# One more tile pair per layer in seven products, token sums built block by block, and 512-column weight tiles moved by 192 bytes

## The chip, the core and the metric

The kernel runs on one core of one Trainium2 chip. The metric is the device time of one execution in microseconds. The engines are TensorE (PE in the profile, with its weight loads as PEld), VectorE (DVE), ScalarE (ACT), GpSimd (POOL) and the DMA queues, most of them issued by SyncE (SP). A difference of about 1% (10 us) is what a measurement of this kernel can tell from no change.

## The reference

A causal decoder trunk of two layers over 512 tokens of width 1024, in float32. What is computed in layer i:

```python
z = rmsnorm(h, norm_mix_pre[i])
z = mlstm_mixer(z, ...) if i == 0 else swa_sink_mixer(z, ...)
h = h + rmsnorm(z, norm_mix_post[i])
z = conv_ffn(rmsnorm(h, norm_ffn_pre[i]), f_w_up[i], f_conv_w[i], f_conv_b[i], f_w_down[i])
h = h + rmsnorm(z, norm_ffn_post[i])

def conv_ffn(h, w_up, conv_w, conv_b, w_down):
    gate, val = jnp.split(h @ w_up, 2, axis=-1)          # 2 x 2816 columns = 2 x 22 tiles of 128
    gp = jnp.pad(gate, ((0, 0), (CONV_W - 1, 0), (0, 0)))
    gate_c = conv_b + sum(conv_w[j] * gp[:, j:j + S] for j in range(CONV_W))
    return (jax.nn.silu(gate_c) * val) @ w_down
```

The mLSTM mixer projects q, k, v, an output gate and head gates, runs a chunked recurrence and projects out. The attention mixer is grouped-query attention in a window of 128 tokens, with 16 query and 2 key heads.

## The kernel before

**Precision.** Every float32 matmul is made as three passes over a split of both operands: w = w_hi + w_lo and z = act_hi + act_lo, each half rounded to float32r, and w_hi z_hi + w_hi z_lo + w_lo z_hi summed in PSUM. ACT makes each hi (a cast), DVE each lo (a subtraction with both inputs in SBUF). `act_hi` and `act_lo` hold the normed and transposed tokens, [128, 8, 512].

**Weights.** SP loads tiles of 128x1024 into four buffers `raw`; ACT and DVE split them into eight slots of `w_hi` and `w_lo`. The list `SLOT` gives the slot of each tile g, and counting semaphores (`w_hi_done`, `w_lo_done`, `w_used`) keep the order. Between `w_lo` and `act_hi` lies a tile `skew` of 48 floats, so that everything above it stands 192 bytes off the 512-byte grid of the weights. All loops are written out in order; no planner places work.

**Matmuls of 512 columns.** `project` (L1825 to L1833, weights stationary, tokens moving) in its full width, `first_units` (L1851 to L1869), `v_unit` (L1894 to L1917), `out_part` (L2014 to L2029) and `down_part` (L2111 to L2118), the last three with weights moving. In the loop of the down projection the stationary operand is `hid_pair`, which lies in slot 2 of the same weight tiles; in its last four tiles it is `act_hi` and `act_lo`. The halves of `project` and all of the seven products have 256 columns.

**The up projection** makes, for each of 22 tiles f, a pair: gate tile and value tile. The first four pairs are plain (`PLAIN = 4`): pairs 0 and 1 for the first 256 tokens, then for the last 256 (eight half units), pairs 2 and 3 in units of 512 columns. The other 18 pairs (`SEVENS`) take seven products each (L2090 to L2109): the 2x2 blocks over (input half, token half) of gate and value are formed by a Strassen scheme. A product is 4 steps of k x 3 passes with 256 columns. They need
- sums of tokens `t1` to `t4` (`t_sums`), made by DVE from `act_hi` and `act_lo` in `first_sums` (L1500 to L1511) and `last_sums`, then split as `t_hi_form` (ACT, `form_hi`) and `t_lo_form` (DVE, `form_lo`, L1524);
- sums of weights, made by POOL in `weight_sums` (L604 to L618): four additions of 128x512, with both inputs in SBUF. For pair (m, t) they wait until PE is done with the tiles whose slots they overwrite: `pool.wait_ge(w_used, m * 4 + counted(up + 2 * t - 3))`. ACT and DVE split them (`raw_hi`, `sum_hi`; `raw_lo`, L1533 and L1536, `sum_lo`, L1549).

**Order around a pair.** ACT and DVE work on pair f while PE makes the products of the next one. `conv` or `conv_taps` are two DVE operations (L1468, L1472) from PSUM, `silu` (L853) is ACT's, `gated_val` (L1482) writes `hid`. In `seven(m, t, nm, nt, pm, pt)` ACT's order is: `raw_hi` of the next pair, `part 0`, `silu` of the previous pair, `raw_hi`, `part 1`, `part 2`, `sum_hi`, `part 3`, `sum_hi`. PE waits for `part 0` before its third product, `part 1` before its fourth, `part 2` before its fifth.

Of the kernel before, what the change touches and what calls it, by code (L numbers as in the profile page):

```python
# [24 lines left out]
F32 = mybir.dt.float32  # L25
# [5 lines left out]
P = 128  # L31
# [8 lines left out]
def trunk(nc, x, x_turned, columns, m_w_in, m_gate_bias, m_w_out, a_w_in, a_sinks, a_w_out,  # L40
# [34 lines left out]
    PLAIN = 4  # L75
    SEVENS = FT - PLAIN
    SKEW = 48
    HT = S // 2
    QW = KT // 2 * P
    assert FT % 2 == 0 and PLAIN == 4  # L80
# [7 lines left out]
    FFN_SLOTS = [4 + n % 4 for n in range(2 * PLAIN)]  # L88
    FFN_SLOTS += [(0, 1, 6, 7)[n % 4] for n in range(2 * SEVENS)] + [n % 2 for n in range(FT - TAIL)]
# [8 lines left out]
    DMAS[G_GATE] = 0  # L98

# [20 lines left out]
    with ExitStack() as ctx:  # L120
# [6 lines left out]
        def below():  # L127
# [22 lines left out]
        KB = 256  # L150
# [10 lines left out]
        t_last_sum = nc.alloc_sbuf_tensor_at("t_last_sum", [P, D], F32, offset=t_last_at + 4 * D)  # L161
        t_early = nc.alloc_sbuf_tensor_at("t_early", [P, 4, D], F32R, offset=arena_at + 4 * 48 * KB)
# [59 lines left out]
        hid = arena[:, 0:44 * KB].rearrange("p (f t) -> p f t", f=FT)  # L222
        cv = arena[:, 44 * KB:48 * KB].rearrange("p (b t) -> p b t", b=2)
# [6 lines left out]
                              for w in (w_hi, w_lo))  # L230

# [9 lines left out]
        wg_pack = w_hi[:, 7].rearrange("p (k c) -> p k c", k=KT)  # L241
# [39 lines left out]

        t_sum, t_form_hi, t_form_lo = sem("t_sum"), sem("t_form_hi"), sem("t_form_lo")
# [107 lines left out]
        def unit(slot):  # L390
            return (w_hi[:, slot].rearrange("p (k c) -> p k c", k=KT),
                    w_lo[:, slot].rearrange("p (k c) -> p k c", k=KT))
# [154 lines left out]
        def _(pool):  # L547
# [81 lines left out]
            nc.gpsimd.tensor_tensor(w_lo[:, s], raw[:, s % 4], w_hi[:, s].bitcast(F32),  # L629
                                    ALU.subtract).then_inc(w_lo_done, 1)  # L630
# [11 lines left out]
        def _(act):  # L642
# [7 lines left out]
            def split_hi(g):  # L650
# [4 lines left out]
                nc.scalar.copy(w_hi[:, s], raw[:, s % 4]).then_inc(w_hi_done, 1)  # L655
# [45 lines left out]
            for k in range(KT):  # L701
# [4 lines left out]
                if k >= 1:  # L706
                    act.wait_ge(raw_in[m], 16)
                    nc.scalar.copy(w_hi[:, m, cols], raw[:, m, cols]).then_inc((even_hi, w_hi_done)[k % 2], 1)
# [125 lines left out]
            norm_pre(2 * NB - 1, NB - 1)  # L834
# [1540 lines left out]
```

## Time and profile before

| | us |
|---|---|
| three runs | 1044.77, 1052.29, 1052.50 (median 1052.29) |
| the profiled execution, its own time | 1044.88 |
| its span (first to last instruction) | 1043.0 |
| PE busy | 1034.1 (99%) |
| DVE busy | 712.0 (68%) |
| ACT busy | 540.8 (52%) |
| POOL busy | 288.1 (28%) |

In 40 slices PE is at nine tenths or more in all but the last one. DVE is at eight to nine tenths in the slices in which the up projections run, at three to seven tenths elsewhere. The granted TensorE clock is full throughout (mean 0.999). A matmul row's duration includes its pipeline, so the distance from start to start is the measure of what one costs. The profiled execution is 7.4 us shorter than the median of the three runs and agrees with the shortest of them.

### The profile page before, as it was taken

To read this page: it belongs to the slowest core of one execution; us is meant where nothing else is said; L and a number is where in the kernel's file an instruction comes from. 1 tells how busy PE (TensorE), PEld (TensorE's weight loads), DVE (VectorE), ACT (ScalarE), POOL (GpSimd) and SP (SyncE) were. 2 spreads that over 40 slices of the span, in tenths; PEclk is the share of its full clock that TensorE was granted. 3 is DMA by queue.
4 is the path that set the end of the run, shared out by engine and by line. 5 is a ranking of instruction groups with operands and counts; after the bars stand their busy time and mean duration, and the time that the engine had idled before them with its cause. 6 is when DMAs were issued, how large, how long until landed. Compare 5 with 4: busy or idle time off the path is not lost.

```text
span 1043.0 us, 18760 instructions
## 1 busy us (share of the span) xinstructions
PE 1034.1 (99%) x6822; PEld 921.7 (88%) x6822; DVE 712.0 (68%) x1013; ACT 540.8 (52%) x971; POOL 288.1 (28%) x195
## 2 busy tenths in 40 slices
PE   9999999999999999999999999999999999999997
PEld 7788888888999999988889987789899999988886
DVE  7534659768888898633357578668889888933344
ACT  6510446445666666533255366765566666633342
POOL 1000121002766766100000032300576667500000
PEclk9999999999999999999999999999999999999999
DMA  9243226432433443223273462113244344222342
GB/s 283 94 135 92 81 81 222 93 90 81 121 96 106 121 120 97 69 97 101 101 186 77 122 142 82 21 41 103 60 121 118 90 113 121 83 92 88 101 141 81
DMA packets 154828, 111.18 MB, mean 107 GB/s; under 512 B 35536, under 2 KB 140144, under 8 KB 154784
## 3 DMA queue, kind: packets, MB, share of 16 engines
q1 hardware_dynamic: 153776, 107.41, 35.8%
q0 software_dynamic: 864, 2.92, 0.9%
q8 instruction: 28, 0.46, 0.2%
q10 hardware_dynamic: 144, 0.26, 0.1%
q14 instruction: 16, 0.13, 0.0%
HBM read 106.87 MB, written 2.13 MB: 105 GB/s over the span
## 4 chain that ended last, share of the span: by engine, by line
PE 92%; DVE 5%; ACT 1%; SPq 1%; issue 1%; DMA 0%; DVEq 0%; ACTq 0%
PE ps L2083 11%; PE ps L2085 11%; PE ps L2084 11%; PE ps L2117 8%; PE ps L2118 8%; PE ps L2116 8%; PE ps L1830 5%; PE ps L1832 5%; PE ps L1831 5%; PE ps L2022 2%; PE ps L2024 2%; PE ps L2023 2%; PE ps L1913 1%; PE ps L1911 1%; PE ps L1912 1%; PE ps L2213 1%
## 5 line engine op out<-in xcount | busy, mean ns | idle before, releaser
L1830 PE MATMUL ps<-act_hi,w_hi 128*128 128x256 f32 (+1 forms) x440 | 144.0, 327 | 1.4 <-DVE act_lo L1161 1.4
L1832 PE MATMUL ps<-act_hi,w_lo 128*128 128x256 f32 (+1 forms) x440 | 141.7, 322 | 0.0
L1831 PE MATMUL ps<-act_lo,w_hi 128*128 128x256 f32 (+1 forms) x440 | 141.7, 322 | 0.0
L1626 DVE TENSOR_TENSOR w_lo<-raw,w_hi 128x1024 fp32r<-128x1024 f32 x32 | 39.2, 1225 | 117.6 <-ACT w_hi L960 117.6
L2083 PE MATMUL ps<-act_hi,w_hi 128*128 128x256 f32 x432 | 119.3, 276 | 0.0
L2085 PE MATMUL ps<-act_hi,w_lo 128*128 128x256 f32 x432 | 119.3, 276 | 0.0
L2084 PE MATMUL ps<-act_lo,w_hi 128*128 128x256 f32 x432 | 119.3, 276 | 0.0
L613 POOL TENSOR_TENSOR sums<-raw 128x512 f32<-128x512 f32 x36 | 49.6, 1377 | 231.1 <-PE ps L1832 139.0
L2116 PE MATMUL ps<-w_hi 128*128 128x512 f32 x288 | 112.1, 389 | 0.0
L2117 PE MATMUL ps<-w_lo,w_hi 128*128 128x512 f32 x288 | 112.1, 389 | 0.0
L2118 PE MATMUL ps<-w_hi,w_lo 128*128 128x512 f32 x288 | 112.1, 389 | 0.0
L1549 DVE TENSOR_TENSOR w_lo<-sums,w_hi 128x1024 fp32r<-128x1024 f32 x72 | 88.0, 1224 | 25.0 <-POOL sums L618 25.0
L655 ACT CAST w_hi<-raw 128x1024 fp32r<-128x1024 f32 x66 | 68.2, 1045 | 65.8 <-PE ps L1913 24.9
L960 ACT CAST w_hi<-raw 128x1024 fp32r<-128x1024 f32 x32 | 33.8, 1055 | 122.0 <-PE ps L2118 122.0
L1830 PEld LDWEIGHTS ps<-act_hi,w_hi 128*128 128x128 f32 x440 | 82.7, 188 | 11.0 <-DVE act_lo L1161 1.8
L1111 DVE TENSOR_TENSOR w_lo<-raw,w_hi 128x1024 fp32r<-128x1024 f32 x65 | 78.4, 1218 | 19.2 <-ACT w_hi L655 19.1
L1832 PEld LDWEIGHTS ps<-act_hi,w_lo 128*128 128x128 f32 x440 | 82.7, 188 | 7.6
L1831 PEld LDWEIGHTS ps<-act_lo,w_hi 128*128 128x128 f32 x440 | 82.7, 188 | 7.5 <-issue 0.2
L887 ACT CAST w_hi<-sums 128x1024 fp32r<-128x1024 f32 x72 | 75.7, 1055 | 20.2 <-POOL sums L616 20.0
L2084 PEld LDWEIGHTS ps<-act_lo,w_hi 128*128 128x128 f32 x432 | 81.1, 188 | 0.1
L2083 PEld LDWEIGHTS ps<-act_hi,w_hi 128*128 128x128 f32 x432 | 81.1, 188 | 0.1
L2085 PEld LDWEIGHTS ps<-act_hi,w_lo 128*128 128x128 f32 x432 | 81.1, 188 | 0.0
(267 smaller groups left out, 2819.9 us busy)
## 6 DMA issues: line engine op xcount, KB each, us to landing
raw<-in_f_w_up SPq DMA_DIRECT2D x88, 512.0 KB, 4.5
raw<-in_f_w_down SPq DMA_DIRECT2D x44, 512.0 KB, 3.3
raw<-in_m_w_in SPq DMA_DIRECT2D x23, 512.0 KB, 4.2
raw<-in_m_w_out SPq DMA_DIRECT2D x8, 512.0 KB, 3.3
raw<-in_a_w_in SPq DMA_DIRECT2D x16, 256.0 KB, 4.3
raw<-in_a_w_out SPq DMA_DIRECT2D x16, 256.0 KB, 4.9
h<-in_x SPq DMA_DIRECT2D x4, 512.0 KB, 7.5
h<-in_x_turned SPq DMA_DIRECT2D x3, 512.0 KB, 6.8
```

Of the source, the lines that this page charges most:

```text
L887: ins = nc.scalar.copy(forms_hi[t][:, fs], sums[:, t, fs])
L1111: nc.vector.tensor_tensor(w_lo[:, s], raw[:, s % 4], w_hi[:, s].bitcast(F32), ALU.subtract).then_inc(w_lo_done, 1)
L1549: ins = nc.vector.tensor_tensor(lo, sums[:, t, fs], hi.bitcast(F32), ALU.subtract)
L1830: nc.tensor.matmul(dst, uh[:, k], zh, start=(k == 0), stop=False)
L1831: nc.tensor.matmul(dst, uh[:, k], zl, start=False, stop=False)
L1832: ins = nc.tensor.matmul(dst, ul[:, k], zh, start=False, stop=(k == KT - 1))
L2083: nc.tensor.matmul(dst, uh, zh, start=(start and k == 0), stop=False, skip_group_check=not start)
L2084: nc.tensor.matmul(dst, uh, zl, start=False, stop=False, skip_group_check=not start)
L2085: ins = nc.tensor.matmul(dst, ul, zh, start=False, stop=(k == KT // 2 - 1), skip_group_check=not start)
L2116: nc.tensor.matmul(dst, hi[:, bs], w_hi[:, s, hs], start=start, stop=False)
L2117: nc.tensor.matmul(dst, hi[:, bs], w_lo[:, s, hs], start=False, stop=False)
L2118: return nc.tensor.matmul(dst, lo[:, bs], w_hi[:, s, hs], start=False, stop=stop)
```

## The change

Four things are changed together.

- `PLAIN` is 3: pair 3 of each layer joins the seven products. The slots of the FFN tiles are laid out anew: the one plain pair of full width goes to slots 0 and 1. PE's first `seven(1, 1)` stands ahead of the loop and waits for each token form alone (`form_made`), where it had waited for all four.
- The token sums start from sums z = hi + lo of blocks of 128 tokens (`z_sum`, DVE; for the third block ACT copies z from PSUM). Three of the four are made earlier, in the norm stage of layer 0 and the attention of layer 1. `first_sums` is then two DVE operations of 128x1024 instead of four, `last_sums` three instead of four. In layer 1, `z_sum(0)` stands right behind `moved_rest`, ahead of `inverse(15)`.
- The order on ACT and DVE ahead of the first seven products is changed: forms in the order t3, t2, t4, t1, interleaved with the split of the weight forms; the lo split of pair 3 and the convolution of pair 2 ahead of the products go; the latter's taps (`conv_taps(1, 0)`) now stand behind `sum_lo(1, 1, 1)`, and so behind all forms.
- `skew` goes. `w_hi` is followed by 256 floats and `w_lo` by 48, so that the tokens keep their 192 bytes; the tiles in `STEPPED`, which are used by matmuls of 512 columns (all projections of layer 0, the first four tiles of both out projections, the plain full-width pair, the last four down tiles) are written and read 48 floats higher (`on_hi`, `on_lo`, `held(g)`).

```diff
-    PLAIN = 4
+    PLAIN = 3
+    STEP = 48
+    FORM_ORDER = [2, 1, 3, 0]
...
+    STEPPED = set(range(G_MOUT + KT // 2)) | set(range(G_AOUT, G_AOUT + KT // 2))
+    for l in range(2):
+        STEPPED |= set(range(G_UP[l] + 4, G_UP[l] + 2 * PLAIN)) | set(range(G_DOWN[l] + FT - TAIL, G_DOWN[l] + FT))
...
-        w_hi = sb("w_hi", [P, 8, D], F32R)
-        w_lo = sb("w_lo", [P, 8, D], F32R)
-        sb("skew", [P, SKEW])
+        held_hi = sb("held_hi", [P, 8 * D + KB], F32R)
+        held_lo = sb("held_lo", [P, 8 * D + STEP], F32R)
+        on_hi, on_lo = (w[:, STEP:8 * D + STEP].rearrange("p (s f) -> p s f", s=8) for w in (held_hi, held_lo))
...
             def ffn_sums(l):
-                with pool.Fori(PLAIN // 2, FT // 2) as m:
+                weight_sums(l, 1, 1)
+                with pool.Fori(2, FT // 2) as m:
...
# ACT, FFN
-                conv(0, 0)
-                hi_pair(0, 2)
-                conv(0, 1)
-                hi_pair(0, 3)
-                for j in range(4):
-                    form_hi(j)
-                conv(1, 0)
-                raw_hi(PLAIN // 2, 0, False)
-                raw_hi(PLAIN // 2, 0, True)
-                sum_hi(PLAIN // 2, 0, 0)
-                sum_hi(PLAIN // 2, 0, 1)
-                conv(1, 1, False)
-                seven(PLAIN // 2, 0, PLAIN // 2, 1, 1, 1)
+                hi_pair(2)
+                conv(0, 0)
+                conv(0, 1)
+                form_hi(2)
+                raw_hi(1, 1, False)
+                raw_hi(1, 1, True)
+                form_hi(1)
+                sum_hi(1, 1, 0)
+                form_hi(3)
+                form_hi(0)
+                sum_hi(1, 1, 1)
+                conv(1, 0, False)
...
+            def z_sum(b, k0=0, k1=KT):
+                at = slice(k0, k1), slice(b * P, (b + 1) * P)
+                nc.vector.tensor_tensor(z_block(b)[:, k0:k1], act_hi[:, at[0], at[1]].bitcast(F32),
+                                        act_lo[:, at[0], at[1]].bitcast(F32), ALU.add).then_inc(z_summed, 1)
...
# DVE, first_sums and last_sums
-                    nc.vector.tensor_tensor(t3, h1b, l1b, ALU.add)
-                    link(nc.vector.tensor_tensor(t4, h0b, l0b, ALU.add))
-                    link(nc.vector.tensor_tensor(t1, t4, h0a, ALU.subtract))
-                    nc.vector.tensor_tensor(t1, t1, l0a, ALU.subtract).then_inc(t_sum, 1)
+                    z_sum(NB - 1)
+                    nc.vector.tensor_tensor(t1, zb0, za0, ALU.subtract).then_inc(t_sum, 1)
...
-                    link(nc.vector.tensor_tensor(t4, h1a, t2, ALU.subtract))
-                    nc.vector.tensor_tensor(t4, t4, l1a, ALU.add).then_inc(t_sum, 1)
+                    nc.vector.tensor_tensor(t4, za1, t2, ALU.subtract).then_inc(t_sum, 1)
...
# DVE, FFN
                 first_sums()
                 conv(0, 0)
-                lo_pair(0, 2)
+                lo_pair(2)
                 conv(0, 1)
-                lo_pair(0, 3)
                 last_sums()
-                for j in range(4):
-                    form_lo(j)
-                conv(1, 0)
-                raw_lo(PLAIN // 2, 0, False)
-                raw_lo(PLAIN // 2, 0, True)
-                sum_lo(PLAIN // 2, 0, 0)
-                sum_lo(PLAIN // 2, 0, 1)
-                seven(PLAIN // 2, 0, PLAIN // 2, 1, 1, 1, True)
+                form_lo(2)
+                raw_lo(1, 1, False)
+                raw_lo(1, 1, True)
+                form_lo(1)
+                sum_lo(1, 1, 0)
+                form_lo(3)
+                form_lo(0)
+                sum_lo(1, 1, 1)
+                seven(1, 1, 2, 0, 1, 0, True)
+                seven(2, 0, 2, 1, 1, 1)
...
# DVE, attention of layer 1
                 if m == A_PAIRS - 2:
                     moved_rest(FIRST_MOVED)
+                    dve.wait_ge(moved_lo, len(MOVED))
+                    z_sum(0)
...
# PE
-                pe.wait_ge(t_form_lo, 4 * (l + 1))
-                with pe.Fori(PLAIN // 2, FT // 2) as m:
+                seven(1, 1, 4 * l)
+                with pe.Fori(2, FT // 2) as m:
```

## Rows read from the trace of the kernel before

**Rows 1.** The page: busy shares, and the chain by engine.

```profile
PE 1034.1 (99%) x6822; PEld 921.7 (88%) x6822; DVE 712.0 (68%) x1013; ACT 540.8 (52%) x971; POOL 288.1 (28%) x195
...
PE 92%; DVE 5%; ACT 1%; SPq 1%; issue 1%; DMA 0%; DVEq 0%; ACTq 0%
```

**Rows 2.** Timeline of PE: start (us), duration (us), engine, line, operation, count.

```profile
56.60 0.39 PE L1911 MATMUL ps<-w_hi,act_hi 128*128 128x512 f32 x1
...
59.35 0.39 PE L1911 MATMUL ps<-w_hi,act_hi 128*128 128x512 f32 x1
...
239.52 0.39 PE L1830 MATMUL ps<-act_hi,w_hi 128*128 128x512 f32 x1
...
261.92 0.28 PE L2083 MATMUL ps<-act_hi,w_hi 128*128 128x256 f32 x1
...
271.77 0.28 PE L2083 MATMUL ps<-act_hi,w_hi 128*128 128x256 f32 x1
...
433.61 0.39 PE L2116 MATMUL ps<-w_hi 128*128 128x512 f32 x1
...
526.11 0.39 PE L2116 MATMUL ps<-w_hi 128*128 128x512 f32 x1
```

**Rows 3.** Waits of PE: engine, tile, line, releaser: us in total, times, longest.

```profile
PE ps L1830 <- DVE act_lo L1161: 1.4, 1, 1.4
```

**Rows 4.** Timeline of DVE ahead of the first seven products, layer 0.

```profile
241.01 0.69 DVE L1482 TENSOR_TENSOR arena<-ps,arena 128x512 f32<-128x512 f32 x1 [0.70 <-ACT arena L853]
...
249.26 2.36 DVE L1524 TENSOR_TENSOR t_early<-arena,t_early 128x1024 fp32r<-128x1024 f32 x2
251.54 2.32 DVE L1524 TENSOR_TENSOR t_third<-g_pre,t_third 128x1024 fp32r<-128x1024 f32 x1
...
256.01 0.74 DVE L1468 SCALAR_TENSOR_TENSOR arena<-ps,vecs,arena 128x511 f32<-128x511 f32 x1
...
260.31 0.68 DVE L1533 TENSOR_TENSOR w_lo<-raw,w_hi 128x512 fp32r<-128x512 f32 x1
```

**Rows 5.** Timeline of POOL: its first batch of weight sums, start of the next.

```profile
250.97 1.81 POOL L613 TENSOR_TENSOR sums<-raw 128x512 f32<-128x512 f32 x1 [78.70 <-PE ps L1832]
...
254.97 2.27 POOL L616 TENSOR_TENSOR sums<-raw 128x512 f32<-128x512 f32 x1
257.19 1.29 POOL L618 TENSOR_TENSOR sums<-raw,sums 128x512 f32<-128x512 f32 x1
262.16 2.26 POOL L613 TENSOR_TENSOR sums<-raw 128x512 f32<-128x512 f32 x1 [3.67 <-PE ps L1832]
```

**Rows 6.** Chain of waits into the fourth product: start, us, what.

```profile
263.97 0.76 DVE arena L1472
...
265.29 0.60 ACT w_hi L877
265.89 0.28 ACT parts L899
...
266.21 0.38 PE ps L2083
```

**Rows 7.** Timeline of the attention around the last moved block, layer 1.

```profile
680.62 0.15 DVE L1731 TENSOR_TENSOR arena<-arena 128x4 f32<-128x4 f32 x1
...
681.07 1.89 POOL L635 TENSOR_TENSOR arena<-arena 128x1024 f32<-128x1024 f32 x1 [3.15 <-DVE arena L1732]
...
683.02 1.09 PE L2226 MATMUL ps<-ident,arena 128*128 128x128 f32 x8
```

**Rows 8.** Timeline of PE: its first work, and the first four 512-column matmuls.

```profile
1.12 4.21 PE L1846 MATMUL ps<-arena 128*128 128x128 f32 x18 [1.12 <-DVE arena L1168]
5.04 1.88 PE L1858 MATMUL ps<-act_hi,w_hi 128*128 128x512 f32 x4
```

**Rows 9.** Windows after the last matmul: busy PE, PEld, DVE, ACT, POOL; granted clock; DMA.

```profile
1037.90:1040.70 2.80, 0.00 (x0) 0.00 (x0) 2.10 (x3) 1.00 (x4) 0.00 (x0) 1.00 0.27 110
1040.90:1043.00 2.10, 0.00 (x0) 0.00 (x0) 0.00 (x0) 0.00 (x0) 0.00 (x0) 0.50 0.60 228
```

More of the change, by code:

```diff
@@ L1089, in _ @@
                 if w == ("turn", NB - 2, 1):
+                    for half in range(2):
+                        n = TURNS.index(("turn", NB - 2, half))
+                        act.wait_ge(t_lo, n + 1)
+                        nc.scalar.copy(z_block(NB - 2)[:, 4 * half:4 * half + 4],
+                                       ps[:, turn_bank(n)].rearrange("p (k t) -> p k t", t=P))\
+                            .then_inc(z_copied, 1)
                     split_hi(G_UP[1] + 2)
@@ L1824, in _, with project @@
         def _(pe):
-            def project(slot, bank, lo=0, hi=S, ks=range(KT)):
-                uh, ul = unit(slot)
+            def project(g, bank, lo=0, hi=S, ks=range(KT)):
+                uh, ul = by_tile(g)
                 for k in ks:
@@ L1857, in first_units @@
                     cs = slice(cols + n * P, cols + (n + 1) * P)
-                    nc.tensor.matmul(ps[:, n], w_hi[:, m, cs], act_hi[:, k], start=(k == 0), stop=False)
+                    nc.tensor.matmul(ps[:, n], on_hi[:, m, cs], act_hi[:, k], start=(k == 0), stop=False)
                 pe.wait_ge(x_lo, k + 1)
@@ L1861, in first_units @@
                     cs = slice(cols + n * P, cols + (n + 1) * P)
-                    nc.tensor.matmul(ps[:, n], w_hi[:, m, cs], act_lo[:, k], start=False, stop=False)
+                    nc.tensor.matmul(ps[:, n], on_hi[:, m, cs], act_lo[:, k], start=False, stop=False)
                 pe.wait_ge(*((even_lo, m + 1) if k % 2 == 0 else (w_lo_done, counted(m))))
@@ L2111, in down_part, with seven, form_made @@
-                def down_part(s, pair, b, half, start, stop):
+                def seven(m, t, forms_made=None):
+                    n = l * SEVENS + t - PLAIN
+                    first, last = slice(0, HT), slice(HT, S)
+                    gate, val, other = 2 * t, 2 * t + 1, 6 + t
+                    def form_made(j):
+                        if forms_made is not None:
+                            pe.wait_ge(t_form_lo, forms_made + j)
+                    pe.wait_ge(hid_done, m * 2 + (l * FT + t + 1))
+                    pe.wait_ge(f_lo, m * 6 + 3 * n + 1)
+                    product(t, 0, z1a, val, last, True).then_inc(product_mm, 1)
+                    pe.wait_ge(f_lo, m * 6 + 3 * n + 3)
+                    form_made(1)
+                    product(t, 3, t3, gate, first, True).then_inc(product_mm, 1)
+                    pe.wait_ge(part_done, m * 8 + 4 * n + 1)
+                    form_made(2)
+                    product(t, 4, t2, val, last, False).then_inc(product_mm, 1)
+                    pe.wait_ge(part_done, m * 8 + 4 * n + 2)
+                    form_made(3)
+                    product(t, 2, t4, gate, first, False).then_inc(product_mm, 1)
+                    pe.wait_ge(part_done, m * 8 + 4 * n + 3)
+                    pe.wait_ge(w_lo_done, m * 4 + counted(up + 2 * t + 1))
+                    form_made(4)
+                    product(t, 5, t1, val, last, False).then_inc(product_mm, 1)
+                    product(t, 1, z2a, other, first, True).then_inc(product_mm, 1)
+                    pe.wait_ge(part_done, m * 8 + 4 * n + 4)
+                    product(t, 6, z2b, val, last, False).then_inc(w_used, 2)
@@ L2112, in down_part @@
+                seven(1, 1, 4 * l)
+                with pe.Fori(2, FT // 2) as m:
+                    for t in range(2):
+                        seven(m, t)
+                def down_part(g, pair, b, half, start, stop):
                     bs = slice(b * P, (b + 1) * P)
```

162 lines of the change are left out of this document (77 added, 85 removed).

## The prediction, made before the changed kernel ran

> **What bounds the kernel now.** I read the page first: PE is busy 99% of the span and carries 92% of the chain of waits [rows 1]. So a part of the change counts in full if it shortens PE's stream, or if it makes PE wait. The list of PE's waits says how much waiting there is to win: its largest entry is 1.4 us [rows 3], so almost nothing. Next I read PE's timeline by start times, because durations overlap. The plain full-width pairs of layer 0 take 239.52 to 261.92 for 96 matmuls, 233.3 ns each for 512 columns. Seventeen pairs in seven products take 271.77 to 433.61 for 1428 matmuls, 113.3 ns each for 256 columns; a product of 12 is 1.36 us and a pair 9.52 us. The loop of the down projection takes 433.61 to 526.11 for 408 matmuls, 226.7 ns; `v_unit` takes 56.60 to 59.35 for 12, 229.2 ns [rows 2]. Last I read DVE, POOL and the chain at the start of the seven products of layer 0 [rows 4 to 6], where the change takes time away. The first pair there takes 261.92 to 271.77, 9.85 us [rows 2]: 0.33 us of waiting. The place is already just in time.
>
> **Terms that shorten PE.** *One more pair in seven products:* 48 x 233.3 ns = 11.20 us become 9.52 us, 1.68 us per layer, 3.4 us in all. *The step of 192 bytes:* 512 columns cost 226.7 ns where stationary and moving tile both lie on the weights' grid (down loop), and 229.2 to 233.3 ns where one lies 192 bytes off it [rows 2]. The step puts both at the same offset. No row has weights and tokens at equal offsets; I take 226.7 ns as the nearest, with no gain at all as the other end. Stationary weights: first units 96, gates 16, q/k units 96, output-gate units 168, together 376 x 6.6 ns = 2.5 us; the plain pair left in each layer, 96 x 6.6 ns = 0.6 us. Moving weights: `v_unit` 192, half of both out projections 192, four down tiles per layer 192, together 576 x 2.5 ns = 1.4 us. The last output-gate unit runs in halves of 256 columns; I cost it at nothing, since no row has that case (bounds: 0.3 us either way). Sum: 3.4 + 2.5 + 0.6 + 1.4 = 7.9 us won. The step's own writes and reads are the same instructions at other addresses.
>
> The page "TensorE: Matmul & The Clock Gate" of the Trainium skill (Part 2, step by step) speaks against the step: it gives PE two independent SBUF read ports and says that loading the next weights takes no bandwidth from the running matmul. By that, addresses would not matter and the step would bring nothing. The rows disagree, with 226.7 against 233.3 ns for the same shape.
>
> **The handoff to the seven products.** This is where I expect the time to go. Today PE reaches them 22.4 us after the last half unit (239.52 to 261.92). After the change one pair stands between, 48 x 226.7 ns = 10.9 us: PE is there at 250.4 and at its fourth product, three products on, at 254.5. That product waits for `part 1` on ACT, which stands behind `silu(1, 0)`, which waits for DVE's taps `conv_taps(1, 0)`, the last thing in DVE's new queue.
>
> DVE's queue from `gated_val(0, 1)` on: today that row ends at 241.70 [rows 4]. The cast of the plain pair now stands ahead of the first convolution, so DVE no longer waits for it; I take 1.1 us earlier (bounds 0 and 1.1), 240.6. Then follow t2, t3, t4, four form splits, one raw split and two sum splits: ten full tiles, each 1.14 us from start to start when alone (two in 249.26 to 251.54); one half tile, 0.6 us; two taps, 1.5 us. Together 13.5 us, ending at 254.1. That alone would be about on time.
>
> But POOL's sums fall into it. POOL's four additions start as PE frees the slots: at 250.97 today, and again at 262.16 [rows 5]. Now the first batch waits for the last half unit (239.5) and the second for the plain pair (250.4), so both fall into DVE's queue. Side by side they are slow: with POOL at work, two form splits take 251.54 to 256.01, 2.24 us each [rows 4], and POOL's addition takes 2.27 us instead of 1.29 us [rows 5]. So one POOL addition holds a two-input DVE operation up by 1.10 us; the taps, which read PSUM, are not slowed (0.74 us at 256.01, inside POOL's 254.97 to 257.24). Eight additions, the first of them nearly over when DVE comes: 7 x 1.10 + 0.2 = 7.9 us. The taps end at 240.6 + 13.5 + 7.9 = 262.0. From the end of the taps to PE's fourth product today is 1.5 us: 263.97 + 0.76 = 264.73 to 266.21, over `silu`, a half cast and `part 1` [rows 6]. So PE's fourth product starts at 263.5 instead of 254.5: 9.0 us of waiting per layer. The form splits are late too, but lie inside this. After it DVE has one pair's work per 9.52 us as today, and I expect no second wait. Layer 1 runs the same lines in the same order, so the same 9.0 us. In all 18.0 us, less the 0.33 us that layer 0 has now.
>
> What the change removes does not help: two of the four operations of `first_sums` end before the taps' input is there; `lo_pair` of pair 3, one sum and the convolution of pair 2 are already left out of the queue above. The `z_sum` made early lie in DVE's idle time of the norm stage of layer 0 and cost nothing; if that cover were gone, 1.2 us each. SP issues the same loads in the same order; each waits for a `w_lo_done` that comes earlier or at the same time.
>
> **The wait in layer 1's attention.** `z_sum(0)` stands ahead of `inverse(15)`. Today this runs at 680.62, POOL's scaling follows to 682.96, and PE's transposes start at 683.02, right behind it [rows 7]. So PE waits for the whole of `z_sum(0)`, 1.2 us and its semaphore, 1.3 us (bounds 0 and 1.3). Queued behind it on DVE is the norm of block 2, for which PE waits next; it shifts by the same amount.
>
> **The clock.** After PE's last matmul starts at 1037.3 the granted clock is still 1.00 up to 1040.7 and then 0.50 (1.2 GHz) [rows 9]. The gap before the fourth product is 263.5 minus three products' end at about 256.6, some 7 us, twice as long, so the clock should fall in it, once per layer. What it costs on the way back: nothing at least. At most what the run's start shows: PE works from 1.12, and its first four 512-column matmuls from 5.04 still take 1.88 us [rows 8], where four at full rate would take 3 x 0.233 + 0.39 = 1.09; some 5.5 us at half rate lose 2.7 us. I take 2.0 us per layer, 4.0 us, nearer the upper end, since PE resumes from a full stop.
>
> **Sum.** 1044.88 - 7.9 + 18.0 - 0.3 + 1.3 + 4.0 = 1060.1 us. This stands on the profiled execution's own time; on the median of the three runs, 7.4 us higher, it would be 1067.5. Nothing in the profile explains the two levels, so the forecast goes by the lower, and the range takes in the other.
>
> **Rivals.** *A: the handoff holds.* If DVE keeps 1.14 us per tile beside POOL, or POOL gets out of its way, the taps end at 254.1, and PE waits 255.6 - 254.5 = 1.1 us per layer, with no gap long enough for the clock: 1044.88 - 7.9 + 2.2 - 0.3 + 1.3 = 1040.2 us, faster. It decides at taps done by 253.0. For it: the list of operations fits without POOL. Against it: the rows of DVE and POOL side by side. Chance 0.22. *B: half of it.* POOL's second batch comes behind DVE's queue, or yields to it, so only the first counts: 9.0 - 4.4 = 4.6 us of waiting per layer, without the clock: 1044.88 - 7.9 + 9.2 - 0.3 + 1.3 = 1047.2 us. Against it: the batch is released by PE at 250.4, long before DVE is through. Chance 0.18. *C: the step does nothing* (the rule of the Trainium skill's page above): 4.5 us less won, everything else as forecast, 1064.6 us. Against it: the two spacings above. Chance 0.10. *D:* the whole forecast without the clock's fall, 1056.1 us, belongs to the forecast. Forecast with D: 0.50.
>
> **Range and chances.** The cases run from 1040.2 to 1064.6 us, and 7.4 us more if the runs stand on the upper level. 1042 to 1069 leaves out the lower part of A and the top of C. About 1% of the time, 10.4 us, is what a measurement can tell from no change. Most of the forecast and C lie beyond it: slower 0.49. A (-4.7 us) and B (+2.3 us) lie within it, and so does a forecast with smaller waits: within 1% 0.42. Faster by more than 1% would need more than all terms won without any wait (-8.2 us), so only a shift between the two levels gives it: 0.09.
>
> **What would show it.** In the changed kernel's trace: 512-column matmuls of the q/k and output-gate units 227 ns apart (233 would be C); the first pair in seven products of each layer taking 18 to 21 us instead of 9.5, with PE waiting for ACT's `part 1` behind DVE's taps; DVE's form splits at 2.2 us each beside POOL's eight additions; the granted clock at one half for a few microseconds behind that gap; and PE's transposes in the last attention step 1.3 us late. The prediction is wrong if the first pair takes under 12 us, or if DVE's splits stay at 1.2 us with POOL at work.

## The result, and the profile after

The changed kernel is slower, and the forecast's main mechanism is what made it so. The compared runs of the changed kernel took 1069.45, 1069.18, 1061.30 and 1069.69 us (median 1069.32), those of the kernel before 1052.24 us at the median; the ratio is 1.0137, with a 95% interval of 1.0079 to 1.0195. Forecast were 1060.1 us on the lower level of the kernel before, and a range up to 1069. The run times of both kernels come in levels, groups some 7 us apart; the profiled execution took 1069.45 us of its own time (span 1067.7), so it is one of the upper ones.

From the page of the changed kernel, busy shares and the chain by engine; they answer to [rows 1].

```profile
PE 1042.0 (98%) x6894; PEld 936.1 (88%) x6894; DVE 731.7 (69%) x1021; ACT 548.2 (51%) x986; POOL 306.3 (29%) x203
...
PE 89%; DVE 7%; ACT 2%; issue 1%; SPq 1%; DMA 0%; POOL 0%; DVEq 0%; ACTq 0%
```

The totals move little. PE's waits show the place at once. Against one entry of 1.4 us [rows 3] there are now (tile, line and releaser; us in total, times, longest):

```profile
PE ps L2112 <- ACT parts L918: 11.5, 2, 6.5
PE ps L2112 <- DVE held_lo L1573: 4.2, 2, 2.1
...
PE ps L2268 <- POOL arena L652: 1.1, 1, 1.1
```

15.7 us in the first pair in seven products of the two layers (6.5 and 5.0 us before the fourth product, 2.1 us in each layer before the second), 1.1 us in the attention. PE's timeline in layer 0 (start, duration, in brackets the idle time before), which answers to [rows 2]: the last plain matmul, the first product, the second, the third, the third's end, the fourth, and the beginning of the next pair.

```profile
248.93 0.39 PE L1862 MATMUL ps<-act_hi,held_lo 128*128 128x512 f32 x1
249.16 0.28 PE L2112 MATMUL ps<-act_hi,held_hi 128*128 128x256 f32 x1
...
252.82 0.38 PE L2112 MATMUL ps<-t_third,held_hi 128*128 128x256 f32 x1 [2.09 <-DVE held_lo L1573]
...
254.31 0.28 PE L2112 MATMUL ps<-t_early,held_hi 128*128 128x256 f32 x1
...
255.55 0.28 PE L2114 MATMUL ps<-t_early,held_lo 128*128 128x256 f32 x1
262.35 0.58 PE L2112 MATMUL ps<-t_last,held_hi 128*128 128x256 f32 x1 [6.52 <-ACT parts L918]
...
269.55 0.28 PE L2112 MATMUL ps<-act_hi,held_hi 128*128 128x256 f32 x1
```

The first pair takes 249.16 to 269.55, 20.4 us, where 9.52 us would do. DVE's timeline in the same stretch answers to [rows 4]: `gated_val(0, 1)`, one sum, forms and sum splits, the taps at the end.

```profile
238.67 0.69 DVE L1513 TENSOR_TENSOR arena<-ps,arena 128x512 f32<-128x512 f32 x1 [0.70 <-ACT arena L872]
...
243.12 2.31 DVE L1544 TENSOR_TENSOR t_last_sum<-z_first,arena 128x1024 f32<-128x1024 f32 x1
245.36 2.31 DVE L1548 TENSOR_TENSOR t_third<-g_pre,t_third 128x1024 fp32r<-128x1024 f32 x1
247.60 1.21 DVE L1560 TENSOR_TENSOR held_lo<-raw,held_hi 128x1024 fp32r<-128x1024 f32 x1
...
249.34 1.21 DVE L1548 TENSOR_TENSOR t_early<-arena,t_early 128x1024 fp32r<-128x1024 f32 x1
...
254.91 2.30 DVE L1548 TENSOR_TENSOR t_early<-arena,t_early 128x1024 fp32r<-128x1024 f32 x1
257.13 2.28 DVE L1573 TENSOR_TENSOR held_lo<-sums,held_hi 128x1024 fp32r<-128x1024 f32 x1
259.33 0.74 DVE L1499 SCALAR_TENSOR_TENSOR arena<-ps,vecs,arena 128x511 f32<-128x511 f32 x1
260.11 0.75 DVE L1503 SCALAR_TENSOR_TENSOR arena<-ps,vecs,arena 128x510 f32<-128x510 f32 x1
```

And POOL's batches, which answer to [rows 5]: first and last addition of each.

```profile
238.59 1.30 POOL L629 TENSOR_TENSOR sums<-raw 128x512 f32<-128x512 f32 x1 [68.53 <-PE ps L1862]
...
244.31 2.28 POOL L634 TENSOR_TENSOR sums<-raw,sums 128x512 f32<-128x512 f32 x1
249.40 2.27 POOL L629 TENSOR_TENSOR sums<-raw 128x512 f32<-128x512 f32 x1 [2.81 <-PE ps L1862]
...
256.09 2.24 POOL L634 TENSOR_TENSOR sums<-raw,sums 128x512 f32<-128x512 f32 x1
```

DVE's 128x1024 operations last 2.3 us as long as POOL is at work (up to 246.6 and from 249.4 to 258.3), and 1.21 us in the pause between at 247.60. Of those beside POOL's second batch only the one at 249.34 keeps its 1.21 us: it began just ahead of POOL, and there POOL's first addition took 2.27 us. The taps, from PSUM, are not slowed. The chain of waits into the fourth product answers to [rows 6]: taps, half a cast, `part 1`, PE.

```profile
260.11 0.76 DVE arena L1503
...
261.43 0.60 ACT held_hi L896
262.03 0.28 ACT parts L918
...
262.35 0.58 PE ps L2112
```

The granted clock, in windows on PE (busy PE with its instructions, clock, DMA): in and behind the gap of layer 0, afterwards, then the same in layer 1.

```profile
259.00:262.00 3.00, 0.00 (x0) 0.51 0.36 106
262.00:265.80 3.80, 3.45 (x16) 0.50 0.72 192
266.00:290.00 24.00, 24.00 (x214) 1.00 0.32 90
...
754.00:760.80 6.80, 3.97 (x18) 0.50 0.56 154
762.00:790.00 28.00, 28.00 (x240) 1.00 0.41 114
```

The last row holds something that was not foreseen. 240 matmuls in 28.00 us, at a full clock and without a wait, are 117 ns each; in layer 0, 214 in 24.00 us are 112 ns (by start times, which count no matmul at the edges twice, 117.8 and 113.3 ns). Layer 1's whole stream runs slower than layer 0's. More on it below. Last, the attention of layer 1, which answers to [rows 7]: `z_sum(0)`, the reciprocal, POOL, PE.

```profile
687.92 1.23 DVE L1141 TENSOR_TENSOR z_first<-act_hi,act_lo 128x1024 f32<-128x1024 f32 x1
...
689.51 1.89 POOL L652 TENSOR_TENSOR arena<-arena 128x1024 f32<-128x1024 f32 x1 [4.41 <-DVE arena L1757]
...
691.46 1.09 PE L2268 MATMUL ps<-ident,arena 128*128 128x128 f32 x8 [1.05 <-POOL arena L652]
```

### The profile page after: what moved, and what is told of

Same layout as the page of the kernel before. It is cut to its first block, busy times and chain, and to the rows that moved or that the text cites. A ratio compares the mean times of both kernels' runs of the same rounds, so it can differ in the third digit from the quotient of the medians.

```text
span 1067.7 us, 19000 instructions
## 1 busy us (share of the span) xinstructions
PE 1042.0 (98%) x6894; PEld 936.1 (88%) x6894; DVE 731.7 (69%) x1021; ACT 548.2 (51%) x986; POOL 306.3 (29%) x203
## 4 chain that ended last, share of the span: by engine, by line
PE 89%; DVE 7%; ACT 2%; issue 1%; SPq 1%; DMA 0%; POOL 0%; DVEq 0%; ACTq 0%
PE ps L2112 11%; PE ps L2113 11%; PE ps L2114 11%; PE ps L2160 7%; PE ps L2159 7%; PE ps L2158 7%; PE ps L1860 4%; PE ps L1862 4%; PE ps L1861 4%; PE ps L2051 2%; PE ps L2053 2%; PE ps L2052 2%; PE ps L1940 1%; PE ps L1941 1%; PE ps L1942 1%; PE ps L2255 1%
## 5 line engine op out<-in xcount | busy, mean ns | idle before, releaser
L1860 PE MATMUL ps<-act_hi,held_hi 128*128 128x256 f32 (+1 forms) x408 | 131.3, 322 | 1.8 <-DVE act_lo L1191 1.7
L1862 PE MATMUL ps<-act_hi,held_lo 128*128 128x256 f32 (+1 forms) x408 | 128.9, 316 | 0.0
L1861 PE MATMUL ps<-act_lo,held_hi 128*128 128x256 f32 (+1 forms) x408 | 128.9, 316 | 0.0
L2114 PE MATMUL ps<-act_hi,held_lo 128*128 128x256 f32 x456 | 127.0, 279 | 0.0
L2113 PE MATMUL ps<-act_lo,held_hi 128*128 128x256 f32 x456 | 127.0, 279 | 0.0
L2112 PE MATMUL ps<-act_hi,held_hi 128*128 128x256 f32 x456 | 127.0, 279 | 0.0
L1651 DVE TENSOR_TENSOR held_lo<-raw,held_hi 128x1024 fp32r<-128x1024 f32 x32 | 39.2, 1225 | 117.7 <-ACT held_hi L978 117.7
L2159 PE MATMUL ps<-held_lo,held_hi 128*128 128x512 f32 x288 | 112.1, 389 | 0.0
L2160 PE MATMUL ps<-held_hi,held_lo 128*128 128x512 f32 x288 | 112.1, 389 | 0.0
L1136 DVE TENSOR_TENSOR held_lo<-raw,held_hi 128x1024 fp32r<-128x1024 f32 x69 | 83.1, 1219 | 18.2 <-ACT held_hi L672 18.1
L2112 PEld LDWEIGHTS ps<-act_hi,held_hi 128*128 128x128 f32 x456 | 86.6, 190 | 0.1
L1860 PEld LDWEIGHTS ps<-act_hi,held_hi 128*128 128x128 f32 x408 | 76.8, 188 | 9.7 <-DVE act_lo L1191 2.1
```

The lines of the kernel that those rows point to most:

```text
L1136: nc.vector.tensor_tensor(lo, raw[:, s % 4], hi.bitcast(F32), ALU.subtract).then_inc(w_lo_done, 1)
L1860: nc.tensor.matmul(dst, uh[:, k], zh, start=(k == 0), stop=False)
L1861: nc.tensor.matmul(dst, uh[:, k], zl, start=False, stop=False)
L1862: ins = nc.tensor.matmul(dst, ul[:, k], zh, start=False, stop=(k == KT - 1))
L2112: nc.tensor.matmul(dst, uh, zh, start=(start and k == 0), stop=False, skip_group_check=not start)
L2113: nc.tensor.matmul(dst, uh, zl, start=False, stop=False, skip_group_check=not start)
```

## The experiments

**POOL out of the way.** In the first two batches of each layer POOL adds 32 of 512 columns; ACT and DVE split whole tiles as ever. The weight sums of two pairs per layer are left out by this.

```diff
-                first, last = slice(0, QW), slice(QW, 2 * QW)
+                first, last = slice(0, w), slice(QW, QW + w)
...
-                weight_sums(l, 1, 1)
-                with pool.Fori(2, FT // 2) as m:
+                weight_sums(l, 1, 1, 32)
+                weight_sums(l, 2, 0, 32)
+                weight_sums(l, 2, 1)
+                with pool.Fori(3, FT // 2) as m:
```

> The changed kernel, but POOL's first two batches of weight sums in each layer add 32 of 512 columns, and the splits of those sums read loaded weights instead (same shapes, so the same DVE and ACT work; the values of two pairs per layer are wrong). Theory (POOL's additions hold DVE's two-input operations up): DVE's form splits come down from 2.3 to 1.2 us, the taps end near 252.6 instead of 260.9, the first pair in seven products takes 10.5 to 11.6 us instead of 20.1 (layer 0) and 20.7 (layer 1), the granted clock stays at 1.00, and the whole gets some 18 to 20 us shorter: 1042 us, or 1049 us on the upper of the two levels. Rival (DVE's queue is too long by itself, or its order puts the taps too late): the first pair stays above 15 us and the whole above 1055 us.

1041.32 us. PE's wait at the fourth product is 1.9 us in both layers together, the clock stays at 1.00 (2.4 GHz), and DVE's queue, with as many operations as before, runs at 1.14 us a tile. Both layers' products run at 113.3 ns. `gated_val(0, 1)`, a form and a sum split, and the taps:

```profile
237.38 0.69 DVE L1519 TENSOR_TENSOR arena<-ps,arena 128x512 f32<-128x512 f32 x1 [0.70 <-ACT arena L875]
...
247.82 1.22 DVE L1554 TENSOR_TENSOR t_early<-arena,t_early 128x1024 fp32r<-128x1024 f32 x1
248.96 1.22 DVE L1580 TENSOR_TENSOR held_lo<-raw,held_hi 128x1024 fp32r<-128x1024 f32 x1
250.09 0.74 DVE L1505 SCALAR_TENSOR_TENSOR arena<-ps,vecs,arena 128x511 f32<-128x511 f32 x1
250.87 0.75 DVE L1509 SCALAR_TENSOR_TENSOR arena<-ps,vecs,arena 128x510 f32<-128x510 f32 x1
```

From the end of `gated_val` to the end of the taps it is 13.55 us here (238.07 to 251.62) and 21.50 us in the changed kernel (239.36 to 260.86): POOL costs 7.95 us. So the order alone does not make the wait; it needs POOL's additions in the queue.

**The taps earlier in the queue.** `conv(1, 0)` on ACT and `conv_taps(1, 0)` on DVE stand right behind `sum_hi(1, 1, 0)` and `sum_lo(1, 1, 0)`; two splits and a form come behind them. The taps at the head of the first `seven` go (not shown).

```diff
                 form_lo(1)
                 sum_lo(1, 1, 0)
+                conv_taps(1, 0)
                 form_lo(3)
...
```

> The changed kernel with the convolution of pair 2 moved: ACT makes its start behind the first half of the weight sums, DVE its taps behind sum_lo(1, 1, 0), ahead of the splits of t4 and t1. POOL's work is as in the changed kernel. Theory (the queue with POOL in it is some 9 us too long, the taps only stand at its end): the fourth product is no longer the late one, but the fifth is, because sum_lo(1, 1, 1) still ends near 259 to 261; the first pair takes 14 to 16 us, no single gap of PE is over 3 us, the clock stays at 1.00, and the whole gets 7 to 10 us shorter, 1052 or 1060 us. Rival (the order alone is at fault): the first pair takes under 11.5 us and the whole 1043 or 1050 us.

1057.94 us. `part 1` is in time, but the operations that now stand behind the taps are late in their turn. The only large wait of PE:

```profile
PE ps L2114 <- DVE held_lo L1573: 5.9, 3, 2.1
```

The wait was shared out over several smaller ones, none over 2.1 us; the first pair takes 14.9 and 14.7 us. The clock fell once (in layer 1) instead of three times; the forecast had it stay. Like the profiled changed kernel, this run has 113.3 ns in most of layer 0 and 117.8 ns in layer 1, so the two compare as they stand: 11.5 us less, forecast 7 to 10. Where the taps stand thus decides about half of the loss, as long as POOL's additions are in the queue.

**Without the step.** Weights of 512 columns at their old place; everything else as in the changed kernel.

```diff
-        on_hi, on_lo = (w[:, STEP:8 * D + STEP].rearrange("p (s f) -> p s f", s=8) for w in (held_hi, held_lo))
+        on_hi, on_lo = w_hi, w_lo
...
-            return [w[:, SLOT[g]] for w in ((on_hi, on_lo) if g in STEPPED else (w_hi, w_lo))]
+            return [w[:, SLOT[g]] for w in (w_hi, w_lo)]
```

> The changed kernel with no tile stepped (held(g) gives the unstepped tile always). Theory (where stationary and moving tile stand to each other sets the cost of 512 columns): matmuls of the q/k and output-gate units go from 227 to 233 ns, those of v_unit to 229, the whole is 4 to 5 us longer, 1066 or 1073 us, and the half units of 256 columns stay as they are in the changed kernel. Rival (addresses do not matter): no difference in either spacing.

1065.93 us, with 113.3 ns in the products of both layers behind the first pair, against 1061.30 of the changed kernel's lowest run: 4.6 us. 512 columns take 233.3 ns here and 227.3 ns in the changed kernel (`project`), and 229.2 and 227.6 ns (`v_unit`). By stages this run is longer than the profiled changed kernel by 1.15 us up to `v_unit`, 0.77 from there to the out projection, 0.20 in that, 0.56 in the plain pairs and 0.31 in the down projections: 3.0 us for the step. 1.1 us more is a fall of the clock in the half units of layer 0, which this run alone has. The remaining 0.5 us can't be placed by a profile, since the lowest run has none. It would fit this run's half units at 117.8 ns in both layers (0.5 us each), less 0.5 us of shorter waiting at the handoff; that is an estimate.

**The kernel before once more.**

> The kernel before, profiled once more. Theory of the two levels (7.5 us apart): PE's unbroken stream of 256-column matmuls runs at 113.3 or at 117.8 ns each, fixed at its start; one layer's 1512 matmuls at 117.8 ns cost 6.8 us. If this execution stands near 1052 us, one layer's seven products are at 117.8 ns; if near 1045 us, none is. Rival (something outside PE's stream, such as launch or loading): an execution at 1052 us has 113.3 ns in both layers.

1058.40 us, the top of its levels. Windows on PE in the middle of each layer's seven products, first of the profile shown before, then of this one (columns as above):

```profile
280.00:400.00 120.00, 120.00 (x1061) 1.00 0.41 112
770.00:890.00 120.00, 120.00 (x1061) 1.00 0.39 106
```

```profile
280.00:400.00 120.00, 120.00 (x1022) 1.00 0.38 105
770.00:890.00 120.00, 120.00 (x1022) 1.00 0.37 105
```

The same instructions, no wait, a full clock, and 117.8 instead of 113.3 ns from start to start. One layer's products are 1512 matmuls, so 6.8 us (7.2 for the 1596 of the changed kernel). The expectation had the value fixed at the stream's start, and that failed: in layer 0 the products began at 113.3 ns and went to 117.8 ns behind a pause of 0.2 us before the fourth product.

```profile
265.65 0.28 PE L2085 MATMUL ps<-t_early,w_lo 128*128 128x256 f32 x1
265.96 0.38 PE L2083 MATMUL ps<-t_last,w_hi 128*128 128x256 f32 x1
```

The profile shown before has the same pause, and its stream stays at 113.3 ns behind it. The two spacings explain the levels, and 42 later runs of the kernel before bear it out: 11 lie at 1044.8 to 1046.4, 19 at 1051.0 to 1053.3, and 12 at 1058.3 to 1060.2, for none, one or both layers at 117.8 ns (the assignment of runs without a profile is read from their time).

**POOL's first batch early.** Pair 3's weight sums go to a free piece of the arena, so POOL need not wait for PE's last half unit; and `z_sum(0)` stands in DVE's idle time one block later.

```diff
+        first_made = arena[:, 28 * KB:36 * KB].rearrange("p (f c) -> p f c", f=4)
...
-                pool.wait_ge(w_used, m * 4 + counted(up + 2 * t - 3))
+                if not early:
+                    pool.wait_ge(w_used, m * 4 + counted(up + 2 * t - 3))
...
-                weight_sums(l, 1, 1)
+                weight_sums(l, 1, 1, True)
...
+                if w == ("y", NB - 2):
+                    dve.wait_ge(moved_lo, len(MOVED))
+                    z_sum(0)
```

> The changed kernel with two edits, full result. (a) POOL's first batch of weight sums (pair 3) is written to a free piece of the arena instead of the weight slots, so that it need not wait for PE's last half unit and runs ahead of DVE's form splits; (b) z_sum(0) in layer 1's attention stands in DVE's idle time behind the pair before it. Theory (POOL's eight additions beside DVE's queue make the handoff late): four of the eight leave the queue, the taps come some 5 us earlier, PE waits some 2 us per layer at its fourth product instead of 6.7, the granted clock does not fall, and the 1.2 us of the attention go: from 1061.3 (the lower level of the changed kernel) to 1061.3 - 2 x 8.5 - 1.2 = about 1043 us if both layers' 256-column stream runs at 113.3 ns, 6.6 us more for each layer in which it runs at 117.8 ns. Rival (only the placing of the taps at the queue's end counts, not POOL): the wait stays near 6 us and the time within 2 us of 1060.

Median 1047.09 us over 10 runs, lowest 1040.18; against the kernel before 0.9953 (0.9904 to 1.0002), which is not clear of no change. Better than expected, since the second batch did not hold DVE up either. DVE's last sum split and first tap, and POOL's first addition of the second batch:

```profile
249.59 1.22 DVE L1578 TENSOR_TENSOR held_lo<-arena,held_hi 128x1024 fp32r<-128x1024 f32 x1
250.72 0.74 DVE L1503 SCALAR_TENSOR_TENSOR arena<-ps,vecs,arena 128x511 f32<-128x511 f32 x1
```

```profile
248.82 3.14 POOL L632 TENSOR_TENSOR sums<-raw 128x512 f32<-128x512 f32 x1 [16.87 <-PE ps L1868]
```

POOL starts at 248.82 and stands 1.9 us longer than the 1.24 us or so that an addition takes alone, until DVE's operations from SBUF are through. Which of the two is held up is thus not fixed: here DVE had the whole run of operations, in the changed kernel they took turns. The same is seen in the run with POOL out of the way, where an addition of 32 columns, 0.25 us alone, began at 248.09 and took 2.19 us. What decides between the two is not shown. PE waits 1.6 us at the fourth product in both layers together. The profiled execution had 117.8 ns in layer 0 (from 273.0 on; between the wait and there it was 113.3).

**Four plain pairs, with block sums and the step.** `PLAIN` back to 4 with the old order ahead of the products; the rest of the change stays, `z_sum(0)` as in the last experiment. (By its "fourth step" the expectation means the fourth plain pair; the step of 192 bytes stays.)

```diff
-    PLAIN = 3
+    PLAIN = 4
-    FORM_ORDER = [2, 1, 3, 0]
+    FORM_ORDER = [0, 1, 2, 3]
...
```

> The change without its fourth step: PLAIN stays 4, with the order of before ahead of the first seven products; the token sums from blocks, the 192 bytes and the later z_sum(0) stay. Full result. Theory (the handoff of the changed order costs everything that the kernel lost, and step and sums are good by themselves): 1044.9 - 4.5 (512 columns at 226.7 to 227.8 ns, two plain pairs per layer instead of one: 0.6 to 1.2 more) - 0.3 = about 1039.5 us where both layers stream at 113.3 ns, 1046 with one and 1053 with both at 117.8 ns. Rival (the block sums or the shifted weights cost something of their own): no faster than before at the same spacing, 1044 to 1046 at 113.3 ns.

Median 1054.07 us over 10 runs, 1053.24 to 1056.26: as the kernel before (0.9998, 0.9954 to 1.0043). PE has no wait at the handoff. But there is one level only, and by the profiled run, the lowest of the ten, it is the one with both layers at 117.8 ns:

```profile
280.00:400.00 120.00, 120.00 (x1021) 1.00 0.39 108
770.00:890.00 120.00, 120.00 (x1021) 1.00 0.39 108
```

1053.24 less 2 x 6.7 us would be 1039.8, as the theory had for 113.3 ns in both layers. So at equal spacing the parts would gain what was expected of them, and something keeps every run from the lower spacing. That it is the step is tested last.

**Other distances between weights and tokens.** The kernel before with 512 or 256 bytes of `skew` (`SKEW` 128 or 64 floats) instead of 192; and the version with the early batch with `STEP` of 32 or 16 floats (128 and 64 bytes).

```diff
-    SKEW = 48
+    SKEW = 128
...
-    STEP = 48
+    STEP = 32
```

> Kernel before with 128 floats (512 bytes) of skew instead of 48: tokens and weights at the same offset on the 512-byte grid, full result. Theory (the spacing of matmuls hangs on the difference of the two offsets): the 512-column matmuls with tokens moving or stationary come down to 226.7 ns (4.6 us less over the run), while the 256-column ones, which have run at 113.3 or 117.8 ns at a difference of 192 bytes, move to another value: bounds 113.3 (then 1040) and 130 ns (17 ns x 3024 matmuls = 50 us more, 1095). If the two values have nothing to do with the offsets, a layer shows 113.3 or 117.8 ns here as well.

> Kernel before with 64 floats (256 bytes) of skew, full result. Theory as for 512 bytes: at this difference the spacing of 256-column matmuls takes one value in both layers, 113.3 ns or less, and the 512-column ones at a difference stay at 229 to 233 ns: about 1045 us. Rival (the two values have nothing to do with the offset): one layer or both at 117.8 ns, 1052 or 1058 us, as in the kernel before.

> The version with POOL's batch made early, with 128 bytes between the grids of weights and tokens instead of 192, full result. So far 256-column matmuls ran at 120.0 ns where both grids agree (0 and 256 bytes), and at 113.3 or 117.8 ns at 192 bytes. Theory (the spacing is set by how the two operands' addresses stand to each other, and 192 bytes is off its best point): at 128 bytes both layers stream at one value of 113.3 ns or less, 1040 us. Rival (the two values are two ways in which the stream can lock in, whatever the distance): a layer at 117.8 ns, 1047 or 1053 us.

> The same with 64 bytes. Theory: one value in both layers, either at most 113.3 ns (1040 us) or, if 64 bytes are too near to 0, up to 120.0 ns (1060 us). Rival: two values again, as at 192 bytes, which is 64 bytes below 256: 1040, 1047 or 1053 us.

1063.70 and 1064.44 us, then 1059.92 and 1056.79 us. Spacing of the 256-column matmuls, the same in both layers of each run: 120.0 ns at 512 and at 256 bytes (and at 0, in the last output-gate unit of the changed kernel, so the distance seems to count modulo 256 bytes), 118.7 ns at 128, 117.8 ns at 64, and 113.3 or 117.8 ns at 192. The window of the run with 512 bytes:

```profile
280.00:400.00 120.00, 120.00 (x1002) 1.00 0.38 105
```

512 columns behave the other way: at 0 and 256 bytes 227 ns, the least that was seen. The expectations of 113.3 ns at 256 and at 128 bytes failed, and the 512 bytes cost more by the products than they won. Of the distances tried, 192 bytes is the best for 256 columns, although not always at its lower value; no distance brought one low value for both layers. Each of the four was run once, so a second value at 64 or 128 bytes is not excluded.

**The plain pairs without the step.** The last two runs keep the step everywhere but in the plain full-width pairs, from which PE enters the seven products.

```diff
-        STEPPED |= set(range(G_UP[l] + 4, G_UP[l] + 2 * PLAIN)) | set(range(G_DOWN[l] + FT - TAIL, G_DOWN[l] + FT))
+        STEPPED |= set(range(G_DOWN[l] + FT - TAIL, G_DOWN[l] + FT))
```

> As the version with four plain pairs, block sums and the step, but the plain full-width pairs of the FFN are written and read at the weights' old offset: PE comes to the seven products from 512-column matmuls at a difference of 192 bytes, as in the kernel before, full result. The stepped version showed 117.8 ns in both layers and ten runs between 1053.2 and 1056.3, never a lower level. Theory (the stream of 256-column matmuls takes its value from how it is entered, and an entry from 512 columns at equal offsets without a wait between locks it to 117.8 ns): low levels appear again, 1053.2 - 13.2 + 1.2 = 1041 us at 113.3 ns in both layers, 1048 with one; the spread is that of the kernel before. Rival (the level has nothing to do with the entry): all runs at 1053 + 1.2 = 1054 to 1057 us.

> The changed kernel with POOL's batch made early and z_sum(0) later, and the plain full-width pair at the weights' old offset, full result. As a candidate for the fastest: it should be faster than the kernel before. Theory (the entry sets the level until a wait of PE resets it): most layers enter at 113.3 ns; its lowest run 1040.2 + 0.6 = 1041 us, the median between 1041 and 1047, lower than the 1047.1 of the same version with the step. Rival (the waits of about 0.9 us at the fourth product reset the level whatever the entry): the median stays at 1047 to 1048 us, and runs spread from 1041 to 1054.

With four plain pairs: median 1042.76 us over 12 runs, eight at 1041.8 to 1042.9 and four at 1048.6 to 1050.9; ratio 0.9925 (0.9892 to 0.9958). With three plain pairs and the early batch: median 1044.45 us, six runs at 1040.3 to 1042.2 and six at 1046.7 to 1048.0; ratio 0.9928 (0.9892 to 0.9965). Both are faster than the kernel before by 0.7%, with intervals clear of no change but less than the 1% named at the start, and by their medians over 2% faster than the changed kernel. The theories had them so (1041 and 1048 us, and a median between 1041 and 1047). The step in those 96 matmuls per layer was worth 0.6 us by itself (21.79 against 22.40 us) and cost 11.3 us at the median, because the stream behind it took 117.8 ns (in both layers of the profiled run, and by their times in the other nine). The stepped and the unstepped version ran on two chips; the kernel before showed all its three levels on each, so the chip does not make the difference. With three plain pairs the medians differ by 2.6 us only, 1047.09 and 1044.45, and both versions have runs at 1040: there a wait of PE in the first pair comes between. In the profiled run with four plain pairs, one layer each:

```profile
280.00:400.00 120.00, 120.00 (x1062) 1.00 0.41 114
770.00:890.00 120.00, 120.00 (x1021) 1.00 0.38 105
```

In its layer 1 the half units ahead of the plain pairs ran at 117.8 ns from their start at 707.82, and so did the products from 744.43 on. All profiles at 192 bytes agree. Where the plain pairs are not stepped, the products begin with the value with which the half units ended: ten layers of five profiles, six at 113.3 and four at 117.8 ns. Where they are stepped, the products begin at 117.8 ns in ten layers of ten, also behind half units at 113.3 ns (six of the ten). Eight of these ten layers had a wait of PE in the first pair; behind it five settled at 113.3 and three at 117.8 ns.

## Why the prediction was right, point by point

**The handoff.** Right, in place, cause and size. Forecast were 9.0 us of waiting and 2.0 us for the clock per layer, in all 22.0 us. The fourth product starts 13.2 us after the first in both layers (249.16 to 262.35, 743.66 to 756.83), where three products at 113.3 ns take 4.1: 9.1 us late. What the first pair and the rest of the stream lose beyond that and the 117.8 ns is 1.8 us in layer 0 and 1.9 us in layer 1, for the clock. Together 21.9 us. The list of waits has less, 8.6 and 7.1 us: in layer 1 the clock fell a first time behind the gap of 2.1 us, which the forecast did not have, and products two and three ran 1.5 us longer inside what would have been waiting. The taps end at 260.86, forecast 262.0, and PE reached the products 1.2 us earlier than forecast as well (249.16, not 250.4), so the distance between the two is as forecast; from the taps to the fourth product it is 1.49 us, forecast 1.5. A part of the wait lies before the second product, behind `sum_lo(1, 1, 0)`; the forecast had all of it before the fourth, which leaves the sum as it is.

**POOL beside DVE.** Right: +1.10 us for an operation of 128x1024 with both inputs in SBUF (2.31 against 1.21 us), forecast 7.9 us in all, shown 8.0 us by taking POOL's work away.

**Rival A** (the handoff holds) was given 1040.2 us. It is not what this kernel does. The run with POOL out of the way, at 113.3 ns in both layers, had 1041.32 us, 1.1 us more, which is mostly the step's smaller gain (below). The version that moves POOL's batch away had 1040.18 us in its lowest run, but it lacks the 1.2 us of the attention that A includes: that it meets A's number is luck. **Rival B** is excluded by POOL's second batch, which ran in turns with DVE in the changed kernel. **Rival C** is excluded by the run without the step: 233.3 against 227.3 ns for the same instruction, and 113.3 to 120.0 ns for 256 columns at different distances. So the conclusion that the prediction drew from the Trainium skill ("TensorE: Matmul & The Clock Gate", Part 2), that addresses would not matter, does not hold here. Whether the read ports of which the page speaks have to do with it, no run shows.

**One more pair in seven products** won what was forecast, less the waiting that comes with it. In a version where the clock stays up (three plain pairs, not stepped), one plain pair and the 19 pairs of layer 0 take 193.15 us, against 193.76 for two and 18 in the run with four plain pairs: 0.6 us less, of the 1.68 forecast, with one gap of 1.0 us in between.

**The step.** The term of 4.5 us was mis-sized: it is 3.0 us, by stages, from the kernel before to the changed kernel as from the run without the step. The stationary part gave 2.2 to 2.4 us, forecast 3.1; the moving part 0.5 to 0.8 instead of 1.4: `v_unit` won 1.6 ns and not 2.5, and the out projections nothing (48.6 us for layer 0's in the kernel before and with POOL out of the way). The last output-gate unit, costed at nothing with bounds of 0.3 us, runs in 256 columns at equal offsets and takes 120 instead of 114 ns, 0.3 us. (The run with POOL out of the way gains 0.7 us more in the first units, but by a start at the higher rate: between 5.1 and 6.4 us PE starts eight matmuls there and five in the two kernels.)

**The attention.** Right: PE's attention part of layer 1 is 1.22 us longer (145.35 to 146.57), forecast 1.3; moved one block later the 1.2 us are gone (145.22).

**The two levels.** Here the prediction said that nothing in the profile explains them, and let the lower one stand. The low run is at 1061.3 us, 16.5 us above the low run of before (forecast 15.2; the step's smaller gain alone makes 1.5). The profiled one had 6.9 us more in layer 1 from the 117.8 ns, and 0.5 us in each layer's half units. With these, one pair, step, attention and handoff make 24.3 of the 24.6 us between the two profiled executions. By their times two more of the four runs lie on the upper level, and that is why the median is 1069.3 us, at the very end of the range. That the range reaches so far is owed to the 7.4 us taken in without a cause; where in the range the median fell is luck. (The terms of the forecast's sum add up to 1060.0, not 1060.1.)

## What to carry to other kernels

Before giving one engine's queue a deadline, look at which elementwise operations of GpSimd fall into it: here, with both inputs in SBUF, the two engines' operations did not overlap but took turns (2.31 us for 1.21), and what counted was where the other engine's work was released. When run times of a kernel without waits come in evenly spaced levels, compare the start-to-start spacing of the same instruction across profiles before looking for a disturbance. And an address change that makes one shape of matmul faster must be tested on the stream that follows it, too.

## What the runs showed of the hardware

- With both operands in float32r, the spacing of matmuls depends on the distance of their SBUF addresses, and 0, 256 and 512 bytes give the same: 512 columns take 226.7 to 227.6 ns there, and 229.2 to 233.3 ns at 192 bytes; 256 columns take 120.0 ns there, 117.8 at 64, 118.7 at 128, and 113.3 or 117.8 at 192.
- At 192 bytes an unbroken stream of 256 columns holds one of two spacings for over a hundred microseconds at a full clock. A wait of PE can change it (117.8 ns before, 113.3 behind the gap at 252.82 in the changed kernel), and so can a pause that no list of waits has. Changes in either direction came behind a single start-to-start distance of 0.20 to 0.34 us (265.96 in the kernel before once more; 277.99 and 766.94 with the taps earlier), and one with nothing over 0.124 us near it (273.0 with POOL's first batch early). The same pause at 266.21 in the first profile changed nothing. An entry from 512 columns at distance 0 gave 117.8 ns in ten profiled layers of ten; from 512 columns at 192 bytes the stream went on as the 256 columns before them had ended. What happens inside the chip stays open; no run here tells it.
- Where DVE and POOL compete, either can be the one that stands: DVE's operations took 2.31 instead of 1.21 us in turns with POOL, and in another version POOL's took 3.14 instead of about 1.3 us while DVE kept its 1.22.
